# One of the MLP's three inner combinations split in the up phase, in a Strassen-type kernel for one hybrid decoder layer

## The reference

```python
x = x + gate1 * mixed
h = rms_norm(x, norm2_g) * (1.0 + scale2) + shift2
x = x + gate2 * (jnp.square(jax.nn.relu(h @ w_mlp1)) @ w_mlp2)     # w_mlp1 (1024, 4096), w_mlp2 (4096, 1024)
```

## Time and profile before

| | us |
|---|---|
| median of 3 runs | 1140.06 |
| lowest, highest | 1136.9, 1142.74 |
| profiled execution, its own time | 1139.7 |
| its span, first to last instruction | 1137.8 |
| busy: TensorE | 1092.3 |
| busy: VectorE | 769.6 |
| busy: ScalarE | 441.9 |
| busy: GpSimd | 248.7 |
| moved by DMA | 151.71 MB |

### The profile page before, as it was taken

How to read it: one execution, slowest core, us unless ns; L and a number is a source line. 1 busy time by engine, 2 the same in 40 slices (tenths; PEclk the granted TensorE clock), 3 DMA queues, 4 the chain that set the end, 5 groups by cost and what they waited for, 6 DMA issues and landing times. The chain is left out here.

```text
span 1137.8 us, 14053 instructions
## 1 busy us (share of the span) xinstructions
PE 1092.3 (96%) x5210; PEld 882.9 (78%) x5210; DVE 769.6 (68%) x1206; ACT 441.9 (39%) x746; POOL 248.7 (22%) x219
## 2 busy tenths in 40 slices
PE   5999999999999999998999999999899899999998
PEld 4678877777778988776788888887678788787787
DVE  5673556565446767799676767677886957848752
ACT  6342334354444335662333323233522514416231
POOL 2011000000001105213222222223223314232231
PEclk9999999999999999998999999999999999999999
DMA  9967333332013013104535353537626345335205
GB/s 272 275 185 259 128 114 111 112 111 74 28 38 122 29 47 93 38 0 144 180 114 191 113 193 112 194 111 251 229 93 226 145 148 187 100 121 222 74 1 148
DMA packets 150932, 151.71 MB, mean 133 GB/s; under 512 B 14116, under 2 KB 124880, under 8 KB 147280
## 3 DMA queue, kind: packets, MB, share of 16 engines
q1 hardware_dynamic: 142800, 122.45, 33.5%
q0 software_dynamic: 8064, 28.36, 7.6%
HBM read 113.04 MB, written 37.75 MB: 133 GB/s over the span
## 5 line engine op out<-in xcount | busy, mean ns | idle before, releaser
L745 PE MATMUL ps<-cmb_hi,wm_hi 128*128 128x512 f32 x880 | 349.2, 397 | 25.7 <-DVE x1t L2162 9.9
L746 PE MATMUL ps<-cmb_lo,wm_hi 128*128 128x512 f32 x880 | 345.3, 392 | 0.0
L747 PE MATMUL ps<-cmb_hi,wm_lo 128*128 128x512 f32 x880 | 345.1, 392 | 0.0
L745 PEld LDWEIGHTS ps<-cmb_hi,wm_hi 128*128 128x128 f32 x880 | 166.8, 190 | 69.4 <-DVE x1t L2162 12.7
L747 PEld LDWEIGHTS ps<-cmb_hi,wm_lo 128*128 128x128 f32 x880 | 166.8, 190 | 35.3
L746 PEld LDWEIGHTS ps<-cmb_lo,wm_hi 128*128 128x128 f32 x880 | 166.9, 190 | 34.5 <-issue 0.5
L745 PE MATMUL ps<-act_hi,w_hi 128*128 128x512 f32 x400 | 162.2, 405 | 3.0 <-DVE act_lo L1688 3.0
L746 PE MATMUL ps<-act_lo,w_hi 128*128 128x512 f32 x400 | 156.7, 392 | 0.0
L747 PE MATMUL ps<-act_hi,w_lo 128*128 128x512 f32 x400 | 156.7, 392 | 0.0
L1398 ACT ACTIVATE wm_hi<-wm_f 128x512 fp32r<-128x512 f32 x128 | 77.3, 627 | 197.7 <-POOL wm_f L715 151.8
L2162 DVE SCALAR_TENSOR_TENSOR x1t<-ps,ada,x1t 128x512 f32<-128x512 f32 x112 | 83.5, 746 | 81.5 <-PE ps L747 81.5
(11 more groups left out here) (200 smaller groups left out, 1413.8 us busy)
## 6 DMA issues: line engine op xcount, KB each, us to landing
raw<-in_w_mlp_dram SPq DMA_DIRECT2D x128, 256.0 KB, 3.9
cmb_f<-h_spill SPq DMA_DIRECT2D x22, 1024.0 KB, 4.9
wada<-in_w_ada_dram POOLq DMA_DIRECT2D x32, 512.0 KB, 5.0
h_spill<-stage SPq DMA_DIRECT2D x16, 768.0 KB, 6.3
w_raw<-in_w_in_dram SPq DMA_DIRECT2D x18, 512.0 KB, 3.8
ada_rows<-in_w_ada_dram SPq DMA_DIRECT2D x16, 512.0 KB, 7.4
h_spill<-stage SPq DMA_DIRECT2D x32, 256.0 KB, 3.3
h_spill<-stage SPq DMA_DIRECT2D x16, 512.0 KB, 6.7
```

What stands on the lines that cost most here:

```text
L745: pe.matmul(bank, wh, hi, start=first, stop=False, skip_group_check=onto)
L746: pe.matmul(bank, wh, lo, start=False, stop=False, skip_group_check=onto)
L747: return pe.matmul(bank, wl, hi, start=False, stop=last, skip_group_check=onto)
```

## The change

T2 leaves the set of combinations that are stored in float32 and split in the down phase. Instead:

- In the up phase ScalarE's `hidden_hi(p)` copies T2 of pair p to `sums_high` (2 KB a partition, in the bytes of x1's last tile), and VectorE's `hidden_lo(p)` overwrites T2's slot of `stage` with the difference. Both are put one pair later in the queues, behind `e1(p+2)` and behind B11's squares; for pair 14 they are in pair 15, for pair 15 high in pair 17 and low behind the last add of pair 18 (a sixth step of `last_pair`).
- SP's `store_split` stores the two parts to `split_spill`; `store_sums` moves T1 and T3 only. `hidden_sums` waits for the low part's store of the pair before.
- In the down phase T2's two parts (1 MB each) are loaded straight into their places, and TensorE waits for the transfers. `combination_hi` and `combination_lo` of T2 go.
- Tile 7 of x1 is written to `x_spill` before the up phase and read back after the high part of pair 15 is stored; the first add of pair 19 waits for it.
- The early loads of chunk 1's B11 and B21 are issued in pair 18, the third of its chunk, instead of 17.
- For chunk 0, T1 is loaded at the start of pair 15, T3 and T2 right after the weights of pair 17, ahead of the stores of pair 14; B22 and NT4 after them. On ScalarE `e2(15)` is now behind the splits of the weights S2 and S4 of pair 16, and on VectorE T1's low part is behind S1's.
- Pair 16 gets the order of the other chunks' first pairs, and in all of these T3's first half is before the first add.

```diff
-FIRST_LOADS = (B11, B21, T1, T2, T3, B22, NT4)
-STORED = (B11, B22, T1, T2, T3, B21, NT4)
+STORED = (B11, B22, T1, T3, B21, NT4)
+STORED_SPLIT = (T2,)
+PIECES = (B11, B21, T1, T3, B22, NT4)
...
+        sums_high = at("sums_high", [len(STORED_SPLIT), HALF], REG + 28 * KB, F32R)
...
+            def store_split(p):
+                q, j = divmod(p, CHUNK_PAIRS)
+                sp.wait_ge(s_hth, p + 1)
+                sp.dma_start(split_spill[q, 0, :, :, j, :].rearrange("i p n -> p i n"),
+                             sums_high[:, :, :].bitcast(F32)).then_inc(s_sth, 16)
+                sp.wait_ge(s_htl, p + 1)
+                sp.dma_start(split_spill[q, 1, :, :, j, :].rearrange("i p n -> p i n"),
+                             stage[:, SPLIT_SLOTS, :]).then_inc(s_stl, 16)
...
+            sp.wait_ge(s_evb, 2 * N_OUT)
+            sp.dma_start(x_spill[KT - 1], x1t[:, KT - 1, :]).then_inc(s_x1out, 16)
             for p in range(PAIRS):
+                if p == PAIRS - 1:
+                    load_in_place(0, T1)
                 sp.wait_ge(s_wlm, SPLIT[p, A22])
...
                 load_pair(p + 2)
+                if p == PAIRS - 1:
+                    load_in_place(0, T3)
+                    load_in_place(0, T2)
                 if p:
                     store_sums(p - 1)
                     store_b21(p - 1)
...
+                if p + 1 == PAIRS:
+                    store_split(p - 1)
                 if p + 1 < PAIRS:
                     store_b11(p + 1)
+                    store_split(p - 1)
                     if p == PAIRS - 2:
                         hidden_stored(0)
                         load_in_place(0, B11)
                         load_in_place(0, B21)
...
+                if w == PAIRS + 2:
+                    store_split(PAIRS - 1)
+                    sp.wait_ge(s_sth, 16 * PAIRS)
+                    sp.dma_start(x1t[:, KT - 1, :], x_spill[KT - 1]).then_inc(s_x1in, 16)
-                if pp == 1 and q + 1 < CHUNKS:
+                if pp == (1 if q else 2) and q + 1 < CHUNKS:
                     hidden_stored(q + 1 if q else CHUNKS - 1)
...
+            def hidden_hi(p):
+                act.wait_ge(s_tt, 4 * p + 3)
...
+                wait(act, s_sth, 16 * p)
+                act.activation(sums_high[:, :, :], stage[:, SPLIT_SLOTS, :], ACT.Copy).then_inc(s_hth, 1)
...
                     if p + 1 < PAIRS:
                         e1(p + 1)
+                        hidden_hi(p - 1)
...
+            def hidden_lo(p):
+                dve.wait_ge(s_hth, p + 1)
+                dve.wait_ge(s_tt, 4 * p + 4)
+                dve.tensor_tensor(stage[:, SPLIT_SLOTS, :].bitcast(F32R), stage[:, SPLIT_SLOTS, :], sums_high[:, :, :].bitcast(F32),
+                                  ALU.subtract).then_inc(s_htl, 1)
...
                     squared((p + 1) % 2, n_c11(p + 1))
+                    hidden_lo(p - 1)
                     weight_lo(p + 2, A11)
...
+                if (w, i) == (PAIRS + CHUNK_PAIRS - 1, 0):
+                    dve.wait_ge(s_x1in, 16)
                 dve.wait_ge(s_pd, PRODUCT[w, i])
...
+                if pp == 0:
+                    combination_lo(q, T3, 0)
                 add_product(w, 0)
+                if pp == 0:
+                    combination_lo(q, T3, 1)
...
-                if ends:
-                    both_lo(q + 1, T2)
                 add_product(w, 5)
...
                 add_product(w, 6)
                 if w == PAIRS + 1:
+                    next(remains)
+                if w == PAIRS + 2:
                     next(remains)
```

More of the change, by code:

```diff
@@ L429, in hybrid_layer @@
         ST_B22, ST_T1, ST_T2, ST_T3, ST_B21, ST_NT4 = 2, 3, 4, 5, 6, 7
-        def loads_of(q):
-            return FIRST_LOADS if q == 0 else tuple(range(7))
+        SPLIT_SLOTS = slice(ST_T2 + 1 - len(STORED_SPLIT), ST_T2 + 1)
         def piece(q, i, part):
-            return 14 * q + 2 * loads_of(q).index(i) + part + 1
+            return 2 * len(PIECES) * q + 2 * PIECES.index(i) + part + 1
         def halves_of(part):
@@ L595, in _ @@
                 if p == 1:
+                    store_split(0)
                     store_b22(1)
@@ L607, in _ @@
                     store_b22(p)
-            for i in FIRST_LOADS[2:]:
+            for i in (B22, NT4):
                 load_in_place(0, i)
@@ L1515, in _ @@
                         e1(p + 1)
+                        hidden_hi(p - 1)
                 if p:
                     e5(p)
+                if p == 1:
+                    hidden_hi(0)
                 if p and p + 1 < PAIRS:
@@ L1524, in _ @@
                     weight_hi(1, A22)
+                elif p + 1 < PAIRS:
+                    e2(p)
                 else:
-                    e2(p)
+                    hidden_hi(p - 1)
                 if p == PAIRS - 1:
@@ L1578, in _ @@
                     weight_hi(w + 1, S4)
+                if w == PAIRS + 1:
+                    hidden_hi(PAIRS - 1)
             for i, (m, half, bank) in enumerate(((6, 0, TURN_BANK), (7, 1, TURN_BANK + 1), (6, 1, LAST_BANK),
@@ L2022, in hidden_sums @@
                 dve.wait_ge(s_sq, n_b12(p))
+                wait(dve, s_stl, 16 * p)
                 dve.tensor_tensor(stage[:, ST_T1, :], b12, b11, ALU.subtract).then_inc(s_tt, 1)
@@ L2097, in _ @@
             weight_lo(3, A12)
+            hidden_lo(0)
             squared(ST_B22, n_c22(1))
@@ L2131, in _ @@
                     both_lo(0, B21)
-                    both_lo(0, T1)
                     weight_lo(p + 1, S3)
                 weight_lo(p + 1, S1)
+                if p + 1 == PAIRS:
+                    hidden_lo(p - 1)
+                    both_lo(0, T1)
                 weight_lo(p + 1, S2)
@@ L2153, in last_pair @@
                 yield
+                hidden_lo(p)
+                yield
             def add_product(w, i):
@@ L2202, in _ @@
                 add_product(w, 3)
-                if w == PAIRS:
-                    both_lo(0, B22)
-                elif pp == 0:
+                if pp == 0:
                     both_lo(q, NT4)
```

57 lines of the change are left out of this document (27 added, 30 removed).

## The result

| | before | after |
|---|---|---|
| median, us | 1140.12 (22 runs) | 1143.76 (22 runs) |
| lowest, highest | 1136.67, 1142.74 | 1141.14, 1146.79 |
| profiled execution, own time and span | 1139.7, 1137.8 | 1146.2, 1144.4 |
| moved by DMA, MB | 151.71 | 161.16 |

The ratio is 1.0034, 95% interval [1.0023, 1.0045]: 3.6 us slower where 2.4 were forecast, and within the half per cent called the same. The page of after answers to the earlier trace rows: VectorE is 6.7 us less busy, ScalarE 2.6 us more, TensorE 1.6 us more (matmuls at half clock).

A forecast was written before the change was run, and what follows sets the result against it. TensorE, busy 96% of the span, was taken as the bound, so only its gaps could be won. Terms +0.65 - 0.3 + 5.5 - 3.0 = +2.85 us on a span of 1137.8 gave 1142.5 us, range 1134 to 1150.

The forecast's parts named there:

- What can be won: TensorE's gaps at turns 0 to 3, with restarts and half clock: 21 to 22 us, 2% of the span, at most.
- Part 1, steady pairs: Steady up pairs: the added copy and subtraction cost nothing, or 0.75 us if VectorE's idle time were gone.
- Part 1, start: First up pairs: hidden_hi(1) and hidden_lo(1) delay TensorE's gaps at 548.75 and 552.32, +0.65 us, bounds 0 and +1.8.
- Part 2, turn 0: Turn from up to down phase: 1.2 us lost to e2(15)'s store, 1.5 won in small gaps; -0.3, bounds -4 to +3.
- Part 3, turn 1: First new chunk of the down phase: late hidden_lo(15) holds the early loads; +5.5 us, bounds +1 to +12.
- Part 4, turns 2 and 3: Later new chunks: VectorE loses T2's splitting, T1 comes later; -3.0 us together, bounds 0 and 7.9 saved.
- The held store: Rival at turn 0: pair 14's small store overtakes the loads, e2(15) runs at 800; 3.7 us better, 1138.8; chance 0.15.
- Splitting is what costs: Rival: turn 1 loses nothing, turns 2 and 3 lose both gaps (7.9 us); 1132.15; chance 0.12.
- T1's wait: Rival at turns 2 and 3: waiting for T1 replaces T2's splitting entirely; +3.0 us, 1145.5; chance 0.13.
- The slower queue behind the early loads: Rival at turn 1: a MB takes 3.7 to 3.9 us, T1 lands 5 to 6 us later; 1150; chance 0.15.

The follow-up runs named there:

- e5: Not a run: in this place the ScalarE step e5(2) of the up phase, which comes behind e1(3) and releases TensorE at 548.75 in before.
- experiment 3: Against the changed kernel, hidden_hi(1) moved behind e5(2) and hidden_lo(1) behind c22(2) and B22's squares: 1144.03 us, ratio 1.0042.
- kernel 10: kernel 9 with x1's last tile stored behind the weights of pair 2 instead of ahead of them: 1130.4 us, ratio 0.9931.
- kernel 9: Changed kernel with hidden_lo(15) before pair 18's third add, pair 14's stores ahead of T3's and T2's loads, T1 loaded between T2's parts: 1133.22 us, 0.9938.
- after again: A second profile of the changed kernel, unchanged: turn 0 +1.67 us and turn 1 +5.27 us against the first profile of before.
- experiment 2: Against the changed kernel, pair 14's two stores go ahead of the loads of T3 and T2 in up pair 15: 1139.49 us, ratio 1.0006.
- before again: A second profile of the kernel before, unchanged: start +1.80 us and turn 0 -2.49 us against its first profile.
- Experiment 1: Against the changed kernel, hidden_lo(15) moved from behind the last add of pair 18 to before its third add: 1137.06 us, ratio 0.9977.
- experiment 8: Changed kernel with the moves of Experiment 1 to experiment 4, T3's halves behind the first add, T1 loaded between T2's parts for chunks 1 to 3: 1131.9 us, 0.9934.
- experiment 4: Against the changed kernel, VectorE's wait for x1's last tile moved from the first add of pair 19 to the fourth: 1143.05 us, ratio 1.0036.

## Why the prediction was right, and where only by balance

The time was forecast within 1.3 us, and that is in part luck. Three of its terms held; one cost was missed, one came out too low (turn 0) and one too high (turns 2 and 3), and these cancelled in large part. With the means of two profiles of each kernel the stretches give 0.7 + 1.5 + 3.0 + 4.8 - 5.2 = +4.8 us where my sum had +2.85, and the medians +3.6 (interval 2.6 to 5.1).

- **What can be won** (21 to 22 us, only at TensorE's gaps): held. Every stretch without a gap is the same to 0.1 us in all kernels.
- **Part 1, steady pairs:** held, 0.00 us. The subtraction takes 683 ns (681 to 686 in all 16), not the 0.75 us assumed. The contention that the Trainium skill (GPSIMD Engine Reference, Specifications) would allow at the first pairs doesn't appear, but that is a weak test: only the first of the 16 (532.99, 683 ns) overlaps an instruction of GpSimd, and it began before it (533.03).
- **Part 1, start:** +0.65 said. The mean of the two profiles of after less that of before is (2.8 + 2.05)/2 - 1.8/2 = 1.5 us. The order on the queues is as described (e1, `hidden_hi`, e5 0.5 us later), but moving it gained nothing in experiment 3. How much of the 1.5 belongs to the change is open: the awaited store's landing and the clock move this stretch by more from one execution to the next.
- **Part 1, missed.** I gave the spill of x1's tile no line at all: its wait for the last add stands ahead of pair 2's weights on SP's queue. The rule of naming what is queued behind a new wait would have found it. It costs 0.5 us against the first profile of before and 1.1 against the second, counted from the phase's first matmul, and kernel 10, with the spill behind the weights, is 1.0 us better there than kernel 9. Experiment 10 shows the cause.
- **Part 2, turn 0:** the wrong sign, and the mis-sized term is the store that holds e2(15). Taking off the 5.25 us by which after is late by then, A22 starts at 797.7 (before 797.77, +0.8 forecast), e2(15) at 809.0 where 806.7 was forecast, and TensorE goes on at pair 16's third product at 813.0 (810.9 forecast, 809.71 before). In after again e2(15) is 1.6 us later than forecast. So +3.3 instead of +1.2; the small gaps went as said (-1.5), and the turn is at +1.8 instead of -0.3. That the place in the queue is the cause, experiment 2 shows. Which part of the term was too small, the transfers' packets in the trace show: those of the stores have 2048 bytes, those of the loads 8192, and in order of time the 512th of the stores' packets, as many as the awaited store and the one before it hold, begins at 810.2, in before's time 804.9, where I had counted 805.3. So by this count the bytes had their turn when I said, and the landing took 4.1 us (3.5 in after again) instead of 1.4. Against before again the loss of the turn is 4.4 us, so it reaches beyond my upper bound of +3, which was made from a single profile with the half clock in its costly place.
- **Part 3, turn 1:** held nearly row by row. Taking off 7.1 us: early loads at 871.0 (871 said), x1's tile at 872.2 (872.3), B11 at 876.0 (876), TensorE's three gaps 1.08, 1.49 and 0.92 us (1.4, 1.9, 0.9), all with the releasers named. T1 came at 889.6 instead of 891.2, as the last MB before it moved faster than 2.85 us each, so TensorE went on at 897.4 instead of 899.0. The gap of 2.04 us was smaller than said and half clock followed all the same (0.57 in the four us behind it): +4.4 and +5.3 against +5.5. Experiment 1 shows the cause.

```profile
904.40:908.40 4.00, 3.96 (x10) 3.13 (x11) 3.51 (x4) 2.15 (x3) 0.00 (x0) 0.57 0.88 243
```

- **Part 4, turns 2 and 3:** -5.2 instead of -3.0. The half clock of turn 2 went (-1.6) and the second gap of turn 3 too, as said; but the first gap fell from 2.4 to 1.24 us at both turns, where I had 0.3 us. T1's low part is ready 2.2 us earlier than before instead of 1.5, so the wait for T1 takes back less of the gain from T2's splitting than I had said, as in turn 1.

**The rivals.** The held store did not overtake: e2(15) waited for it until 814.25, 9.8 us later than before with the shift taken off. The Trainium skill (DMA: Bandwidth & Descriptors, Queues, rings and completion order) leaves completion out of the order of issue possible; no run here shows it for this store. "Splitting is what costs" is true for 5.2 of 7.9 us at turns 2 and 3 and wrong at turn 1. T1's wait replaces 0.6 to 0.7 us of it a turn (experiment 8), not all. The slower queue behind the early loads did not come: T1 is split 23 us after the last add of pair 18, not 29.

**Where the gain is.** With `hidden_lo(15)`, the stores, T1 and the x1 tile in better places, the same division of T2 gives -3.1, -3.4 and -2.9 us at turns 1 to 3. The change lost on where its new transfers and waits were put, not on what it moved.

## What to carry to other kernels

When work is moved out of a bound engine, list every new wait with everything behind it in its queue, SP's first: here one subtraction five adds too late cost 7 us, one wait in front of a weight load about 1 us, and two stores behind 3 MB of loads 4.5 us, against 9 us gained at turns 1 to 3. Take a second profile of the unchanged kernel before trusting a stretch to a microsecond, and compare the kernels matmul by matmul: medians could not have told the last two versions apart. Begin such a stretch ahead of the half clock, or its slow matmuls are counted as a gain or loss of what follows. Waits in a row on one transfer queue counted once (experiment 4), so shortening the first is worth nothing while the last stays.

## What the runs showed of the hardware

- **The place of the half clock changes from one execution to the next, and matters.** After gaps of 2.2 to 2.3 us TensorE went on at full clock (797.77 in before, 802.94 in after) or at half (798.65 in before again). In front of a wait that ends at a fixed time the slow matmuls cost nothing; behind it 1.6 us. No row tells why it fell here and not there.
- **A store can land some us after its bytes' turn.** With the two split stores behind it in the queue, the store that e2(15) waits for landed 4.1 us after the last packet of its turn by count had begun (810.2 and 814.25 in after); where loads follow it (experiment 2) it took 1.1 us (803.9 and 804.95). From 810 to 812 the queue is busy in full and moves 208 GB/s, against 377 before. Why is open; whether some of the 16 DMA engines lagged isn't shown. The start of e1(3), which waits for another store, lies between 547.6 and 549.2 in the four profiles of the two kernels, with the shift ahead of it taken off.

```profile
807.00:810.00 3.00, 3.00 (x15) 2.49 (x14) 3.00 (x4) 0.00 (x0) 0.00 (x0) 1.00 1.02 377
810.00:812.00 2.00, 1.39 (x7) 0.81 (x5) 0.43 (x1) 0.00 (x0) 0.00 (x0) 1.00 1.10 208
```

- **My count per MB came from a stretch that wasn't full all along.** In after the queue carried 423 GB/s from 890 to 895, against the mean of 362 in the earlier trace rows, at a share of 0.93; T1 was 1.6 us early, as T2's MB in front of it took less. Before itself has 419 GB/s in a full stretch of such loads (the second row below).

```profile
890.00:895.00 5.00, 4.08 (x19) 3.13 (x18) 3.75 (x6) 1.79 (x3) 3.21 (x3) 1.00 1.02 423
```
```profile
805.00:810.00 5.00, 1.54 (x7) 1.01 (x6) 5.00 (x7) 5.00 (x8) 0.00 (x0) 1.00 0.99 419
```
